# Stick-breaking attention in a decoder layer: the product with V and the transposes of a slot change places

## What is computed

```python
def one_block(args):
    q_blk, start = args
    z = jnp.einsum('bhqd,bhkd->bhqk', q_blk.astype(jnp.float32), k32) * scale
    q_pos = start + jnp.arange(Q_BLOCK, dtype=jnp.int32)
    causal = key_pos[None, :] < q_pos[:, None]
    sp = jax.nn.softplus(z)
    neg_log_rem = jnp.where(causal, sp, 0.0)
    after = lax.cumsum(neg_log_rem, axis=3, reverse=True) - neg_log_rem
    log_a = (z - sp) - after
    a = jnp.where(causal, jnp.exp(log_a), 0.0)
    return jnp.einsum('bhqk,bhkd->bhqd', a, v32)
```

## Time and profile before

| | |
|---|---|
| median of 3 runs | 2708.12 us (2707.36 to 2711.16) |
| profiled execution | 2708.43 us |
| its span, first to last instruction | 2706.6 us |
| attention stage within it | 345 to 1110 us |
| TensorE busy | 2525.3 us, 93% of the span |
| VectorE, ScalarE, GpSimd busy | 1297.1, 1140.7, 1247.6 us |
| granted TensorE clock, mean | 0.973 |

### The profile page before, as it was taken

One profiled execution on the slowest core, in us unless ns is written; L12 is line 12 of the kernel. 1 busy time (PEld: TensorE's weight loads), 2 busy tenths in 40 slices (PEclk: granted clock), 3 DMA queues, 4 the chain that ended last, 5 costly groups with the idle time before them and its releaser, 6 DMA issues.

```text
span 2706.6 us, 34870 instructions
## 1 busy us (share of the span) xinstructions
PE 2525.3 (93%) x12272; PEld 2087.3 (77%) x12272; DVE 1297.1 (48%) x1312; ACT 1140.7 (42%) x1857; POOL 1247.6 (46%) x868
## 2 busy tenths in 40 slices
PE   6999879999899999699689999989999999999999
PEld 5888657777777777588568888868887888887887
DVE  4333346766677767435344444524325444442222
ACT  3222256767667677323333333324323333322232
POOL 1122146767667676202464554415636455442332
PEclk9999979999899999899889999999999999999999
DMA  4655573343533521344222122364633222214464
GB/s 159 198 164 166 159 199 98 114 122 96 144 87 99 165 68 52 132 146 163 103 78 93 63 85 85 93 207 146 203 127 109 93 66 84 83 62 163 145 208 136
DMA packets 299865, 336.03 MB, mean 124 GB/s; under 512 B 17888, under 2 KB 239072, under 8 KB 298720
## 3 DMA queue, kind: packets, MB, share of 16 engines
q1 hardware_dynamic: 299744, 334.57, 39.9%
HBM read 240.13 MB, written 94.37 MB: 124 GB/s over the span
## 4 chain that ended last, share of the span: by engine, by line
PE 47%; POOL 2%; DMA 1%; SPq 1%; ACT 0%; DVE 0%; issue 0%; ACTq 0%; DVEq 0%
PE ffn_ps L1672 10%; PE ffn_ps L1674 10%; PE ffn_ps L1676 10%; PE ffn_ps L71 6%; PE ffn_ps L73 5%; PE ffn_ps L72 5%; POOL ffn_A L1610 1%; POOL all_B L1621 1%; SPq L1352 1%; DMA ffn_A_over<-in_w_down 0%; DMA ffn_raw<-in_w_up 0%; POOL ffn_A L1615 0%; DMA ffn_A_over<-hidT 0%; DVE ffn_raw L1519 0%; ACT ffn_A L1435 0%
## 5 line engine op out<-in xcount | busy, mean ns | idle before, releaser
L1610 POOL TENSOR_TENSOR ffn_A<-ffn_raw,ffn_A 128x512 fp32r<-128x512 f32 x264 | 357.9, 1365 | 390.1 <-ACT ffn_A L1404 389.8
L1672 PE MATMUL ffn_ps<-all_B,ffn_A 128*128 128x512 f32 x1232 | 481.3, 391 | 35.4 <-ACT ffn_s L1416 24.6
L1674 PE MATMUL ffn_ps<-all_B,ffn_A 128*128 128x512 f32 x1232 | 480.8, 390 | 0.0
L1676 PE MATMUL ffn_ps<-all_B,ffn_A 128*128 128x512 f32 x1232 | 480.6, 390 | 0.0
L772 DVE TENSOR_TENSOR_SCAN att_stick<-att_z,att_stick 128x128 f32<-128x128 f32 (+5 forms) x192 | 331.3, 1726 | 221.1 <-ACT att_z L684 207.9
L818 POOL TENSOR_TENSOR att_a<-att_a,att_stick 128x128 f32<-128x128 f32 (+5 forms) x192 | 281.8, 1473 | 216.9 <-DVE att_stick L772 216.2
L1615 POOL TENSOR_TENSOR ffn_A<-ffn_A_over,ffn_A 128x512 fp32r<-128x512 f32 x88 | 161.2, 1832 | 352.5 <-ACT ffn_A L1437 352.4
L1672 PEld LDWEIGHTS ffn_ps<-all_B,ffn_A 128*128 128x128 f32 x1232 | 232.3, 189 | 84.9 <-POOL ffn_A L1610 36.6
L71 PE MATMUL ffn_ps<-ffn_A 128*128 128x512 f32 x704 | 276.8, 393 | 16.1 <-POOL ffn_A L1615 16.1
L1547 DVE TENSOR_TENSOR ffn_A<-ffn_A_over,ffn_A 128x1024 fp32r<-128x1024 f32 x88 | 117.5, 1335 | 344.0 <-ACT ffn_A L1435 344.0
L72 PE MATMUL ffn_ps<-ffn_A 128*128 128x512 f32 x704 | 275.8, 392 | 0.0
(11 more groups left out here) (117 smaller groups left out, 5042.5 us busy)
## 6 DMA issues: line engine op xcount, KB each, us to landing
ffn_A_over<-in_w_down SPq DMA_DIRECT2D x88, 512.0 KB, 3.5
att_w_stage<-in_w_in SPq DMA_DIRECT2D x48, 512.0 KB, 4.5
ffn_raw<-in_w_gate SPq DMA_DIRECT2D x22, 1024.0 KB, 6.6
ffn_raw<-in_w_up SPq DMA_DIRECT2D x22, 1024.0 KB, 8.8
hidT<-ffn_s SPq DMA_DIRECT2D x88, 256.0 KB, 2.4
ffn_A_over<-hidT SPq DMA_DIRECT2D x88, 256.0 KB, 3.6
qkv_x_t<-in_x SPq DMA_DIRECT2D x16, 512.0 KB, 4.5
hT_hi<-qkv_hT_hi SPq DMA_DIRECT2D x16, 512.0 KB, 5.3
```

Of the source, the lines that this page charges most:

```text
L1610: nc.gpsimd.tensor_tensor(A[:, j, p, 1, :, :], operand(j, p), A[:, j, p, 0, :, :].bitcast(F32), ALU.subtract).then_inc(lo_done, 1)
L1672: nc.tensor.matmul(ps[:, b, :], A[:, j, p, 0, k, :], B[p][:, 0, k, :], start=first_mm, stop=False, skip_group_check=True)
L1674: nc.tensor.matmul(ps[:, b, :], A[:, j, p, 0, k, :], B[p][:, 1, k, :], start=False, stop=False, skip_group_check=True)
L1676: mm = nc.tensor.matmul(ps[:, b, :], A[:, j, p, 1, k, :], B[p][:, 0, k, :], start=False, stop=last_mm, skip_group_check=True)
```

## The change

In the closing slots `a_times_v` is called ahead of `transposes`. Both keep their waits. The transposes of the slot belong to the next group, so the product doesn't need them. The same is done in the three slots behind the last pair. Planner, buffers and all other engines are as before.

```diff
@@ -943,17 +943,17 @@
                     scores(p, n)
                     for k, i in steps[n]:
                         project_step(p, k, i)
-                    if n >= LAG or not is_first(p):
-                        transposes(p, n - LAG)
                     q, b = at(p, n - LAG)
                     if opens[b] and (n > LAG or not is_first(p)):
                         a_times_v(q, units[b][0] - 1)
+                    if n >= LAG or not is_first(p):
+                        transposes(p, n - LAG)
 
             pairs(pe, body)
             for n in range(NU - LAG, NU):
-                transposes(PAIRS - 1, n)
                 if opens[n]:
                     a_times_v(PAIRS - 1, units[n][0] - 1)
+                transposes(PAIRS - 1, n)
             a_times_v(PAIRS - 1, NG - 1)
```

## The result

The changed kernel takes 2730.85 us (median of 4 runs, 2728.74 to 2732.77), the kernel before 2709.64 beside it (4 runs): 1.0078 of it, 95% interval 1.006 to 1.0095, so some 21 us slower. The profiled executions are 2728.74 and 2708.43 us, 20.3 apart; the sum of the prediction was 19.6.

A forecast was written before the change was run, and what follows sets the result against it. TensorE was taken to set the attention stage's pace, with other engines' round trips between its work. Terms of 4.9 us per pair, 19.4 over four pairs, came to +19.6 with end corrections: 2728.0 us, range 2715.5 to 2737.

The forecast's parts named there:

- Direct effect: Closing slots: the product loses the transposes as cover ahead of it; 2.56 us per pair in eight slots without projections.
- its two parts (0.43 and 0.47): Slot 7: 0.43 us of lost cover, and a late eviction delaying the projection behind it, together 0.9.
- Indirect effect: The transposes' drain and ScalarE's queue behind it start later, delaying evictions, sigmoids and subtractions around slots 7, 13 to 16, 39.
- split of slot 39: ScalarE's 1.06 us weight split stands behind the late copies; transposes of slot 41 start later, +0.7 us.
- Slots 13 to 16: Late sigmoids, subtraction, product of slot 15 and eviction delay slot 16's projection: +1.6 us, ends 0.5 and 1.8.
- product of slot 15: Ready at 600.79, it waits until 601.30 for the late subtraction of slot 14, which ends at 601.17.
- closing slot 33: Closing slot with projections standing between drain and product, so no cover needed: 0 us.
- end of the stage: End of the attention stage: three blocks move behind the second last product, +0.3 us.
- direct only: Rival: later ScalarE and VectorE starts find slack, only lost cover remains; 10.4 us, 2718.8, chance 0.17.
- the seam: Odd seams between kinds of matmul in the attention stage, bounded at -3 to +3 us over 62 closings, taken as 0.
- Clock: Rival: the granted clock also falls mid-pair, say three more times; +8 us over the sum, 2736, chance 0.13.
- No change: Rival: added waits replace waits of the same size, as in slots 22 and 46; 2708.4 us, chance 0.10.

The follow-up runs named there:

- e1_noproj: Kernel before, with the product first only in closing slots without a projection step; 2722.85 us against 2710.98, ratio 1.0047.
- e3_after_early_take: Changed kernel, with ScalarE evicting a finished projection one place earlier, between the sigmoids and copies of its slot; 2711.67 us against the changed kernel's 2730.85.
- e4_before_early_take: Kernel before, with ScalarE evicting a finished projection one place earlier, between the sigmoids and copies of its slot; 2697.39 us against 2710.98, ratio 0.9954.
- e7_after_split_ahead: Changed kernel, with ScalarE's weight split ahead of the copies of the transposes in slots 9 and 39; 2724.25 us against 2730.85.
- e10_after_oadd: Changed kernel, with VectorE's addition that empties the product's accumulator (L793) moved ahead of the scan; 2729.05 us, run once.
- e5_after_cover: Changed kernel, with one projection step of the next slot moved into each closing slot that had none; 2716.05 us, 15 under the changed kernel.
- e9: e5_after_cover with VectorE's addition that empties the product's accumulator (L793) moved ahead of the scan; 2710.82 us, 5 under e5_after_cover.
- e6_before_cover: Kernel before, with one projection step of the next slot moved into each closing slot that had none; 2686.22 us, ratio 0.992.

## Why the prediction was right

**Direct effect.** Right, slot by slot (0.27, 0.49, 0.48 and 0.5 where 0.28, 0.47, 0.47 and 0.43 stood), and `e1_noproj` gives it alone with what hangs on it: +12 for +13. Slot 7 by itself cost 0.6 and slots 8 and 9 0.3, so there the sum was right and its two parts (0.43 and 0.47) were not. The product cannot use the time that the transposes used, since it waits for the same drain and for its later half. One block ahead of a product (slots 1 and 25) costs nothing that the timeline shows.

**Indirect effect.** Right in place and size for the evictions of slots 9 and 16 and for the split of slot 39. `e3_after_early_take` with `e4_before_early_take` and `e7_after_split_ahead` show ScalarE's queue as the path. Slots 13 to 16 cost 1.7 for 1.6. That was pair 1, from which it was worked; in pair 0 the 0.9 of slots 7 to 9 was 0.3.

**A step that was incomplete.** For the product of slot 15 I had only the subtraction as gate (601.17, start 601.30). In fact it waits for L793 as well, 0.41 long and behind that subtraction on VectorE. The wait was in the code (`o_done`) and I did not follow it. It cost little here (0.2 to 0.4 us a time by `e10_after_oadd`), and more in `e5_after_cover`: a closing slot's product starts a chain (transposes, copies, low half, sigmoids, scan, subtraction, addition) that ends at the product two slots later. Where that chain is longer than TensorE's own work in between, cover ahead of the product no longer helps.

**Small terms.** The closing slot 33 costs 0.11 to 0.25, predicted at 0: it stands two behind slot 31. The end of the stage was put at +0.3 for three blocks moved behind the second last product. This is misread: two of the three stood behind it already, and only one block moves. By the last L793 the whole stage ends 20.1 us later, and the scores of slot 46 of pair 3 were 18.6 later, so the end costs 1.5. Little of that is the order's. From the scores of slot 47 to the last L793 it is 13.2 us before and 14.7 after. Of the variants with the product first, `e7`, `e9` and `e10` have 13.3 to 13.4 there, the other three 14.9 to 15.6; of those with the order of before, all six have 14.7 to 16.3. So the order costs 0.1, and the rest is the granted clock, which fell at the end in most runs of either order and not in the kernel before: the second last product takes 5.33 us after and 3.94 before. The stretch view of the kernel after, and of the one before for its end:

```profile
1120.00:1130.00 10.00, 7.11 (x47) 6.53 (x45) 2.60 (x6) 2.12 (x5) 0.00 (x0) 0.83 0.01 2
```
```profile
1100.00:1110.00 10.00, 6.40 (x49) 5.45 (x47) 3.97 (x8) 2.92 (x7) 0.64 (x1) 1.00 0.10 34
```

Two statements of the prediction were off without weight. The product started 0.13 us behind the drain in six slots a pair, not eight; in slots 7 and 31 it was 0.36. And *direct only* less the seam is 2715.8, not 2715.5.

**How near the sum is.** In part this is luck. The slots cost 20.6 us over the four pairs where they were put at 19.3; the starts of pairs 1 and 2 gave 1.8 back and the end took 1.2 more than foreseen, both with the granted clock.

**The rivals.** *Direct only* would have been 2718.8; the eviction waits and `e3_after_early_take` rule it out. *Clock*: the mean granted clock of the attention stage is 0.98 after and 0.97 before, and no middle of a pair fell. One fall came at the end (0.83), where the kernel before had none. A granted clock under 0.95 in a new place was one of my signs of being wrong, but variants with the order of before show the long end as well (see the small terms). It is +1.2, with 0.3 of the end foreseen, and over the starts of pairs 1 and 2 the shift shrank by 0.7 and 1.1 us (in the kernel before the clock was 0.93 and 0.90 in the two stretches of 10 us from 530, in the kernel after 1.00 from 530 to 560). Together these come to about -0.6 us, no cause of the result. The Trainium skill ("TensorE: Matmul & The Clock Gate", Part 4: PE-mode transpose), by which transposes count less as activity, made falls in mid-pair likelier; this trace shows none there. *No change* holds for slots 21 and 45, as the prediction had it. The timeline after shows the same wait as the earlier trace rows:

```profile
635.58 1.13 DVE L784 TENSOR_TENSOR att_aT_lo<-att_tr,att_aT_hi 128x512 fp32r<-128x512 f32 x2
...
636.30 1.12 PE L908 MATMUL att_tr<-all_ident,att_a 128*128 128x128 f32 x8 [1.51 <-DVE att_aT_lo L784]
```

**Why `e6_before_cover` gains twice the waits that I had counted.** The timelines of pairs 1 and 2 say where its 4 us a pair stand. Slots 8 and 9 gain 1.1 together: slot 9's projection no longer waits, since the one before it ends a slot earlier. Slots 13, 19, 37 and 43, each with the slot behind it, gain 0.4 to 0.5. Slots 22 and 46 gain 0.5 each: the wait of the transposes in slot 22 is 0.97 where it was 1.49. I had counted neither slot 9 nor these two.

**What stays open.** A wait shorter than the modelled end of the last matmul has no bracket in the timeline; that I counted too few waits in slots 13 and 37 for this reason is likely but only argued. A second accumulator for the product, which would take the addition off its way altogether, was not tried.

## What to carry to other kernels

Of two pieces of work in an in-order queue, put first the one whose last wait is released earlier, and ask of each what is being drained while it runs: here both wait for one drain, and the piece that needs less of it has to go first, as cover for the other. When a consumer's producer is moved behind a long instruction group, follow the consumer's engine on to what is queued behind it; a third of this loss went through evictions, and 2.6 us of it through a weight split, that have no data in common with what was moved. Before adding cover, look whether the wait belongs to a chain that starts at the same engine: then it moves along.

## What the runs showed that I had not expected

Moving a projection step by one slot changed the order in which SyncE issues two loads and so removed 5.7 us of a 7.57 us stall at the start of the stage (pair 0, slot 7); a planner's slot numbers reach into the DMA queue too. And two small orders on ScalarE and in the planner, with no change in the amount of work, are worth 29 us together (2680.5 against 2709.84), more than the change of the case costs. The stall's part is in it.
